# First attention group of layer 1: four of its projections started in the combining stage, its rotation on VectorE

## The reference

```
h = x * (1 + sc1) + sh1
y = neighbourhood_mixer(h, ...) if i == 0 else gqa_mixer(h, cos, sin, w_qkv, q_gain, k_gain, w_o)
x = layer_norm(ALPHA * x + (1 + g1) * y)
h = x * (1 + sc2) + sh2
y = hierarchical_moe(h, ...)          # 32 experts, 2 of them for each token
x = layer_norm(ALPHA * x + (1 + g2) * y)
```

```
def gqa_mixer(h, cos, sin, w_qkv, q_gain, k_gain, w_o):
    qkv = h @ w_qkv                    # 16 query heads, 4 key heads, 4 value heads, of 64
    q = apply_axial_rope(rms_norm(q, q_gain), cos, sin)
    k = apply_axial_rope(rms_norm(k, k_gain), cos, sin)
    return block_gqa_attention(q, k, v) @ w_o     # softmax over all 1024 keys
```

## Time and profile before

| what | us |
|---|---|
| three executions | 5044.19, 5035.16, 5041.49 |
| the profiled execution | 5040.28 |
| its span on the core | 5038.5 |
| TensorE busy (22530 matmuls) | 4574.7 (91%) |
| VectorE busy | 1867.8 (37%) |
| ScalarE busy | 1124.1 (22%) |
| POOL busy | 539.8 (11%) |

### The profile page before, as it was taken

How to read it: one execution, slowest core, us unless ns; L and a number is a source line. 1 busy time by engine, 2 the same in 40 slices (tenths; PEclk the granted TensorE clock), 3 DMA queues, 4 the chain that set the end, 5 groups by cost and what they waited for, 6 DMA issues and landing times. The chain is left out here.

```text
span 5038.5 us, 54615 instructions
## 1 busy us (share of the span) xinstructions
PE 4574.7 (91%) x22530; PEld 2550.4 (51%) x22530; DVE 1867.8 (37%) x2805; ACT 1124.1 (22%) x1867; POOL 539.8 (11%) x382
## 2 busy tenths in 40 slices
PE   8999989899999889998979999957999897999993
PEld 4555654355565346666444444424666554444441
DVE  3333552433355335454531111132666763111114
ACT  2343221233322113232100000022444410000001
POOL 2221110132111000000000000012221100000001
PEclk9999999999999999999979999978999997999997
DMA  3111053111104411111259999930000025999993
GB/s 96 30 30 30 13 218 111 52 39 30 34 13 184 167 40 41 32 29 54 81 203 339 336 336 335 328 111 13 14 14 35 1 85 190 347 336 336 333 334 142
DMA packets 362693, 691.49 MB, mean 137 GB/s; under 512 B 53659, under 2 KB 139811, under 8 KB 362327
## 3 DMA queue, kind: packets, MB, share of 16 engines
q1 hardware_dynamic: 347143, 632.43, 37.1%
q0 software_dynamic: 14112, 51.39, 2.7%
q10 hardware_dynamic: 1200, 4.24, 0.2%
HBM read 624.20 MB, written 63.82 MB: 137 GB/s over the span
## 5 line engine op out<-in xcount | busy, mean ns | idle before, releaser
L460 PE MATMUL ps<-sb_mixT,sb_work 128*128 128x512 f32 x768 | 359.9, 605 | 9.6 <-ACT sb_x_tok L778 5.5
L460 PE MATMUL ps<-sb_xT,sb_work 128*128 128x512 f32 x768 | 359.2, 604 | 9.6 <-ACT sb_x_tok L778 5.5
L2441 DVE TENSOR_TENSOR sb_work<-sb_work,ps 128x512 f32<-128x512 f32 x66 | 45.4, 688 | 863.0 <-PE ps L2360 863.0
L2360 PE MATMUL ps<-sb_work,sb_xT 128*128 128x512 f32 x800 | 354.0, 596 | 0.8 <-DVE sb_xT L2430 0.8
L2360 PE MATMUL ps<-sb_work,sb_mixT 128*128 128x512 f32 x800 | 353.1, 594 | 0.8 <-DVE sb_mixT L2430 0.8
L1509 PE MATMUL ps<-sb_xT,sb_work 128*128 128x512 f32 x512 | 239.2, 606 | 5.6 <-DMA sb_work<-na_w_qkv 5.6
L2360 PEld LDWEIGHTS ps<-sb_work,sb_xT 128*128 128x128 f32 x800 | 150.4, 191 | 178.3 <-issue 177.1
L2360 PEld LDWEIGHTS ps<-sb_work,sb_mixT 128*128 128x128 f32 x800 | 150.1, 191 | 177.6 <-issue 176.5
L2380 PE MATMUL ps<-sb_mixT,sb_work 128*128 128x512 f32 x528 | 232.1, 592 | 0.9 <-ACT sb_work L2422 0.9
L2380 PE MATMUL ps<-sb_xT,sb_work 128*128 128x512 f32 x528 | 232.1, 592 | 0.9 <-ACT sb_work L2422 0.9
L2436 DVE TENSOR_TENSOR sb_work<-ps,sb_work 128x1024 f32<-128x1024 f32 x66 | 80.8, 1225 | 409.9 <-PE ps L2380 409.9
(11 more groups left out here) (430 smaller groups left out, 7276.0 us busy)
## 6 DMA issues: line engine op xcount, KB each, us to landing
sb_work<-moe_w_up SPq DMA_DIRECT2D x66, 2048.0 KB, 10.4
sb_work<-moe_w_gate SPq DMA_DIRECT2D x34, 2048.0 KB, 10.6
sb_xT<-moe_w_down SPq DMA_DIRECT2D x33, 2048.0 KB, 10.8
sb_mixT<-moe_w_down SPq DMA_DIRECT2D x33, 2048.0 KB, 10.9
sb_work<-ada_w SPq DMA_DIRECT2D x96, 512.0 KB, 6.2
scratch_y<-sb_work SPq DMA_DIRECT2D x82, 512.0 KB, 10.8
sb_xT<-moe_w_gate SPq DMA_DIRECT2D x16, 2048.0 KB, 10.6
sb_mixT<-moe_w_gate SPq DMA_DIRECT2D x16, 2048.0 KB, 10.6
```

Source lines behind the costliest of these rows:

```text
L460: last = pe.matmul(m.ps[:, bank, :], b.w[i][:, k, :], m.xT[:, k, half * HALF:(half + 1) * HALF], start=(k == 0), stop=(k == NK - 1))
L2360: last = pe.matmul(m.ps[:, 2 + 2 * (n % 2) + part, :], b.x_turned[n % 2][:, k * P:(k + 1) * P], w[:, k, :], start=(k == 0), stop=(k == NK ...
L2441: dve.tensor_tensor(b.act[n % 2], b.act[n % 2], m.ps[:, 3 + 2 * (n % 2), :], ALU.mult).then_inc(multiplied, 1)
```

## The change

The combining stage after layer 0 gets the weights of group 0 and starts its projections; the attention stage takes over at piece 4.
- The buffers of the attention stage are laid out by a function of their own, `group_buffers`, with the weights last, so that they lie clear of the gathered rows of the combining stage. The weights of group 0 are loaded in the combining stage, on SP's queue after the four vectors.
- The turns use banks 0 to 3 only, two tiles side by side and two k to a bank. They are copied out after every two tiles: k 0 to 3 by ScalarE, k 4 to 7 by VectorE, four 128x256 copies each. The turn of an even tile waits for the copies of the pair before.
- TensorE's list becomes: turn 0, 1, 2; project 0, turn 3; project 1, turn 4; project 2, turn 5; project 3, turn 6; turn 7. Projections 0 to 3 stay in banks 4 to 7, across the barrier.
- In the attention stage ScalarE evicts these four without a wait; pieces 4 to 7 go to banks 0 to 3 and wait for no eviction.
- For group 0 the rotation is issued on VectorE, each half after its sum of squares; groups 1 to 3 stay on POOL.

The diff, cut to its core:

```diff
+GQA_WIDE, GQA_BEGUN = (GROUP + 2) * HD, NT // 2
+def first_bank(piece):
+    return 4 + piece if piece < GQA_BEGUN else piece - GQA_BEGUN if piece < NT else 7
+def group_buffers(m):
...
+    b.q = [[take(SEQ) for _ in range(2)] for _ in range(2)]
+    b.k2 = [take(SEQ) for _ in range(2)]
+    b.prob = [[take(SEQ) for _ in range(2)] for _ in range(2)]
+    b.probT = [take(SEQ) for _ in range(2)]
+    b.scratch = take(half_tiles * n_norm * HD)
...
+    b.raw = take(NT * GQA_WIDE).rearrange("p (t n) -> p t n", t=NT)
+    b.w = take(NK * GQA_WIDE).rearrange("p (k n) -> p k n", k=NK)
...
 def grouped_query_stage(nc, m, a):
...
-            load_weights(0)
             sp.dma_start(gain_q, a["gqa_q_norm_2"][0].partition_broadcast(P)).then_inc(tables, 16)
...
             def project(g):
...
-                    if piece:
+                    if piece < GQA_BEGUN:
+                        continue
+                    bank = first_bank(piece)
+                    if bank == 7:
                         pe.wait_ge(evicted, piece)
...
-                            last = pe.matmul(m.ps[:, 7, 0:WIDE], m.xT[:, k, n * P:(n + 1) * P], w[:, k, :],
+                            last = pe.matmul(m.ps[:, bank, 0:WIDE], m.xT[:, k, n * P:(n + 1) * P], w[:, k, :],
...
             def evict(g, n):
-                act.wait_ge(projected, GQA_PIECES * g + n + 1)
+                piece = GQA_PIECES * g + n
+                if piece >= GQA_BEGUN:
+                    act.wait_ge(projected, piece + 1 - GQA_BEGUN)
...
+        def rotate(engine, st, g, half):
...
         @block.gpsimd
         def _(pool):
...
-            for g in range(KV_HEADS):
+            for g in range(1, KV_HEADS):
                 for half in range(2):
...
+                    rotate(pool, st, g, half)
...
-            sum_squares(0, 0)
-            sum_squares(0, 1)
+            st = Steps(dve, s["dve_step"])
+            dve.wait_ge(scaled, 1)
+            for half in range(2):
+                sum_squares(0, half)
+                rotate(dve, st, 0, half)
...
 def combine_stage(nc, m, l, columns=None, out=None, first_weights=None):
...
+                load_group_weights(sp, first_weights, group_buffers(m).w, 0, first_loaded)
                 sp.wait_ge(columns_loaded, 64)
...
-            for t in range(NT):
+            def turn(t):
                 pe.wait_ge(normed, t + 1)
+                if t >= 2 and t % 2 == 0:
+                    pe.wait_ge(copied_a, 4 * (t // 2))
+                    pe.wait_ge(copied_b, 4 * (t // 2))
                 for k in range(NK):
...
+            def begin_projection(n):
+                for loaded in first_loaded:
+                    pe.wait_ge(loaded, 16)
+                pe.wait_ge(copied_a, 4 * (n // 2 + 1))
+                pe.wait_ge(copied_b, 4 * (n // 2 + 1))
+                for k in range(NK):
+                    pe.matmul(m.ps[:, 4 + n, 0:GQA_WIDE], m.xT[:, k, n * P:(n + 1) * P], w[:, k, :],
+                              start=(k == 0), stop=(k == NK - 1))
+            for t in range(3):
+                turn(t)
+            for n in range(GQA_BEGUN):
+                begin_projection(n)
+                turn(3 + n)
+            turn(NT - 1)
...
-                    if t == last_half:
-                        copy_out(0)
+                    if t >= 2 and t % 2 == 0:
+                        copy_out(t // 2 - 1)
             if columns is not None:
-                copy_out(1)
+                copy_out(NT // 2 - 1)
```

More of the change, by code:

```diff
@@ L1734, in grouped_query_stage @@
     scaled, v_ready = s["signal_17"], s["signal_18"]
[L1735 to L1743, removed]
-    half_tiles = NT // 2
[L1745 to L1752, removed]
+    count, WIDE, n_norm = GQA_STEPS, GQA_WIDE, GROUP + 1
+    b = group_buffers(m)
+    w, raw, scratch, square, part, q, k2, prob, probT = (b.w, b.raw, b.scratch, b.square, b.part, b.q, b.k2, b.prob, b.probT)
+    half_tiles = NT // 2
     v = [m.v_tok[:, n, :].rearrange("p (t d) -> p t d", d=HD) for n in range(2)]
@@ L1775, in _ @@
             for g in range(1, KV_HEADS):
-                sp.wait_ge(projected, GQA_PIECES * (g - 1) + NT)
-                load_weights(g)
-            sp.wait_ge(projected, GQA_PIECES * (KV_HEADS - 1) + NT)
+                sp.wait_ge(projected, GQA_PIECES * (g - 1) + NT - GQA_BEGUN)
+                load_group_weights(sp, a["gqa_w_qkv_2"][0], w, g, (loaded,) * 3)
+            sp.wait_ge(projected, GQA_PIECES * (KV_HEADS - 1) + NT - GQA_BEGUN)
             load_out_weights(sp, m, a["gqa_w_o_2"][0], s["stored"])
@@ L2544, in experts_stage, with combine_stage @@
             end_stage(nc, m)
-def combine_stage(nc, m, l, columns=None, out=None):
+def combine_stage(nc, m, l, columns=None, out=None, first_weights=None):
     s = m.sem
@@ L2603, in weigh, with copy_out @@
                 act.activation(y[t % 4][0], y[t % 4][0], ACT.Copy, scale=m.gates[:, t, 0:1]).then_inc(weighted, 1)
-            def copy_out(half):
-                act.wait_ge(turned, 4 * half + 4)
+            def copy_out(pair):
+                act.wait_ge(turned, 2 * pair + 2)
                 act.wait_ge(columns_ready, 1)
-                for k in range(0, NK, 2):
-                    dst, src = turned_out(k, half)
+                for k in range(NK // 2):
+                    dst, src = turned_out(k, pair)
                     act.activation(dst, src, ACT.Identity, bias=shift[:, k:k + 1],
@@ L2650, in mix, with copy_out @@
                 dve.wait_ge(var_ready, t + 1)
[L2652 to L2655, removed]
+            def copy_out(pair):
+                dve.wait_ge(turned, 2 * pair + 2)
+                for k in range(NK // 2, NK):
+                    dst, src = turned_out(k, pair)
                     dve.tensor_scalar(dst, src, scale[:, k:k + 1], shift[:, k:k + 1], ALU.mult, ALU.add).then_inc(copied_b, 1)
```

63 lines of the change are left out of this document (49 added, 14 removed).

## The result

The changed kernel took 5006.19 us (median of 4, 4998.81 to 5009.3) against 5041.6 for the kernel before on the same chip: ratio 0.9928, 95% interval 0.9913 to 0.9943. In a second session it took 5003.47 against 5040.73 (five runs and nine), ratio 0.9928 again (0.9914 to 0.9941). The forecast was 5009.4 for a gain of 30.9; measured are gains of 35 and 37.

What follows compares the result with a forecast made beforehand. The path to the first scores, with TensorE underused between the layers, was taken as the bound. Projections 23.8 us earlier, rotation 7.0 and rounding made 30.9 off 5040.3, so 5009.4 us; own case 5003 to 5016, with rivals 5001 to 5024.

Steps and rivals of the forecast that it cites:

- The path: Between the two layers: the program's end moves with the start of the first scores, forecast 30.9 us earlier.
- The combining stage: Between the layers: four pieces of projection put between the turns lengthen the stage by 9.4 us.
- The beat of a piece and a turn: Combining stage: TensorE bounds it, each piece costing 5.43 us and each turn 1.09 at full clock.
- The half clock at piece 0: Combining stage: TensorE's first projection starts at half pace before the clock rises, costing 1.6 us over full pace.
- The DMA delay: Combining stage: weight loads sharing the DMA engines with the gathers delay the stage by 1.5 us.
- The weights: Attention stage: its 7.6 us wait for weights goes; loaded earlier, their own lateness costs nothing.
- the rival with 6.5 us: Combining stage: weights delay the gathers by their whole 6.5 us, or arrive late; +5, 5014 us, chance 12 in 100.
- The projections: Attention stage: pieces 4 to 7, in banks of their own, end 23.3 us after its start, at 3416.6 against 3440.4.
- The rotation: Attention stage, first group: 9.5 us per half on VectorE against POOL's 16.5; the first half stays hidden.
- rival 4: Attention stage: VectorE rotates at POOL's pace; second half +7, first half past its cover by 1; 5018 us, 4 in 100.
- The clock rivals: TensorE at half clock in the combining stage (5034 us, 8 in 100) or both stages (5054 us, 3 in 100).
- The sum: First scores 30.9 us earlier: projections 23.8, rotation 7.0, and rounding.

Runs made afterwards that it cites:

- rotation on POOL: The changed kernel with the first group's rotation, both halves, on POOL again: 5010.1 us, ratio 0.9944 to the kernel before.
- three banks: The changed kernel with the last three turns before the first scores in banks 4, 5 and 6 instead of 7: 5000.08 us, ratio 0.9917.
- one bank: The changed kernel with pieces 4 to 7 all in bank 7, waiting for evictions: 5008.34 us, ratio 0.9936.
- before with rotation on VectorE: The kernel before with only the first group's rotation moved to VectorE, no projections begun early: 5030.26 us, ratio 0.998.
- none begun: The changed kernel with no projections begun in the combining stage, weights still loaded there, eight pieces in eight banks: 5021.53 us, ratio 0.9963.

## Why the prediction was right, step by step

- **The path.** That the first scores carry the whole difference is borne out to 0.01 us by the first pair of profiles (1572.15 and 1572.14 behind them); in the second profile of the changed kernel what is behind them took 1569.87, with the same instructions.
- **The combining stage** was to grow by 9.4 and grew by 5.6 in the first pair of profiles, 6.3 in the second profile of the changed kernel. The mechanism was right, four sizes were not. These are the sizes by the first pair. The beat of a piece and a turn was priced at 5.43 + 1.09 = 6.52 and is 6.03, as the start of one overlaps the end of the other: 2.0 over four. The half clock at piece 0 was charged at 1.6 and cost 0.6: from its start to the next turn's 5.75 us, against 5.16 for the later pieces. That one was luck of the profile: in the second it cost 1.8, and 1.0, 1.8 and 1.8 in the kernels with the rotation on POOL, three banks and one bank, so 1.6 was no bad charge. The DMA delay was 0.9 and not 1.5 (0.2 in the second profile). Turn 2 was 0.3 quicker than charged. Together 3.9, and the stage came out 3.8 shorter than forecast. I priced pipelined instructions by their durations where the starts of neighbours should have been subtracted.
- **The weights.** Their wait (7.6 us) went and nothing came in its place, but with less room than I claimed: alone they were there in 5.3 to 6.5 us, here the first of the three landed 16.7 us after its issue, and SP's wait for all three ended by 3360.5, some 5 us ahead of piece 0 (3365.52). They did not go ahead of the gathers, whose first tile came 0.9 later. The Trainium skill's "DMA: Bandwidth & Descriptors" (Queues, rings and completion order) has each DMA engine take turns between its queues, a packet at a time. The trace agrees with it in both, and the rival with 6.5 us fell. No run takes this wait away by itself; but from "before with rotation on VectorE" to "none begun" the attention stage lost 13.6 us, and the wait of 7.6 and seven evictions at 0.84 make 13.5.
- **The projections** were to end 23.3 us after the stage's start and ended 22.4 after it; own banks are worth 6 (one bank), work moved away 20.8 (none begun). The tables were there 4.8 us after the stage's start (3394.42 to 3399.18), priced at 7.6: before, their issue stood behind the weights on SP. It was covered either way.
- **The rotation** was to take 9.5 and took 9.1 to 9.24; alone in the kernel before it gave 7.03, forecast 7.0. That the first half stays hidden was right for VectorE. On POOL it showed by 1.7; the prediction had this term in its rival 4 alone, at 1.
- **The clock rivals** fell: the granted clock was 0.66 in the window from 3364 to 3368, 1.00 after it, and below it again after the barrier, where pieces 4 to 7 took 22.4 against 4 x 5.16 = 20.6, as charged.
- **The sum**: 30.9 forecast, 35.8 and 34.9 in the two profiles, 35 to 37 in the medians. The difference of 4.9 in the first is the beat (2.0), piece 0's clock (1.0), the DMA (0.6), turn 2 (0.3) and the second stage, which was 1.3 shorter than forecast, 0.9 of it in the projections; these make 5.2, the rest is rounding. Only the beat and the second stage repeat in both profiles. That 5009.4 lies only 3.2 from the median of 5006.19 is in part luck: the forecast started from the profiled run, 1.3 below the median of before, and the gain was missed by 4.5.

## What to carry to other kernels

Find where the bounding engine is idle because another one sets the pace, and move work there whose inputs are ready early: four projections cost 3.9 us there and 20.8 where they stood. When a piece of work leaves its place, ask what it was hiding: the first half's rotation on POOL came out from under it. Price pipelined instructions by the distance of their starts, and measure a form beside the other engine before counting on a split. And where a term hangs on when the clock rises, take a second profile before reading its size off the first.

## What the runs showed of the hardware

From the first scores to the next stage's table load the steady loop of 64 steps took 589.4 to 589.6 us in five profiles, 587.2 and 587.4 in two and 584.9 to 585.7 in five, with the same instructions. The changed kernel alone gave 589.4 and 587.35 (and 1572.14 and 1569.87 from the first scores to the end). The steps that differ stand mostly at the changes of group, where the fixed list puts no projection in, and there the granted clock differs. The same 6 us, 300 to 306 after the first scores, in the kernel before:

```profile
3766.35:3772.35 6.00, 5.18 (x25) 4.47 (x27) 1.37 (x4) 3.26 (x6) 0.00 (x0) 0.51 0.00 0
```

and in the one with three banks:

```profile
3739.39:3745.39 6.00, 4.95 (x54) 4.06 (x56) 2.63 (x6) 3.24 (x6) 0.00 (x0) 1.00 0.01 3
```

Half clock in one, full clock in the other, and the step at this change of group took 12.9 us there and 10.6 here. Of the 4.7 us between the longest and the shortest loop the same kernel shows 2.1; that the rest is scatter too, and not of the edits, is likely, since they touch none of these steps, but not shown. So effects of a few us have to be read from the intervals within a profile.

Beside the gathers, three weight loads kept SP issuing for 12.07 us (3336.15), and 10.7 to 14.4 in the other five profiles that have them there, against 2.41 alone. Here SP had nothing else to issue; a load behind them would have been issued some 10 us late.
